# A two-layer backbone step on one core: half of x loaded behind the first modulation weights, and its squares made after h

## The reference

```python
mod = silu(c) @ w_mod[l] + b_mod[l]           # nine vectors of 1024 for each of the two conditionings
sh1, sc1, g1, ... = split(mod, 9)
h = rmsnorm(x, norm_ffn1) * (1 + sc1) + sh1   # rmsnorm divides by sqrt(mean(x*x) + eps)
x = x + 0.5 * g1 * ((silu(h @ w_gate) * (h @ w_up)) @ w_down)   # 1024 -> 2816 -> 1024
...                                           # mixer (Fourier group and attention), second FFN
```

## Time and profile before

| | |
|---|---|
| median of three timed runs | 2757.12 us |
| the profiled execution's own time | 2753.22 us |
| its span, from the first to the last instruction | 2751.1 us |
| mean granted TensorE clock | 0.993 of full |
| TensorE busy | 2676.0 us (97%) |
| VectorE busy | 2095.2 us (76%) |
| ScalarE busy | 1215.2 us (44%) |
| GpSimd busy | 623.1 us (23%) |
| DMA, mean over the span | 99 GB/s |

### The profile page before, as it was taken

The page is one execution under the profiler, slowest core; times in us unless marked ns, Lnnn a source line. Parts: engine busy times, 40 slices in busy tenths (PEclk is TensorE's granted clock), DMA queues, the critical chain, the costliest instruction groups (busy, mean ns, idle before and its releaser), DMA issues. The chain is left out here.

```text
span 2751.1 us, 44480 instructions
## 1 busy us (share of the span) xinstructions
PE 2676.0 (97%) x17686; PEld 2531.2 (92%) x17686; DVE 2095.2 (76%) x2832; ACT 1215.2 (44%) x1998; POOL 623.1 (23%) x323
## 2 busy tenths in 40 slices
PE   5999999999999999999999999999999999999997
PEld 3999999977799999999989999999778999999997
DVE  6978878766566788887988879887665668786876
ACT  5533425556422553343564335255563235443433
POOL 1322412022000123232321413310220003242240
PEclk9999999999999999999999999999999999999998
DMA  6433232210243243423324242312113422222312
GB/s 234 158 121 127 85 123 73 70 59 21 67 138 107 93 160 120 128 101 106 102 98 154 93 139 98 110 62 75 39 37 101 133 80 85 93 72 75 108 47 77
DMA packets 86445, 272.99 MB, mean 99 GB/s; under 512 B 8736, under 2 KB 10016, under 8 KB 86112
## 3 DMA queue, kind: packets, MB, share of 16 engines
q1 hardware_dynamic: 84800, 265.60, 29.2%
q10 hardware_dynamic: 1440, 4.56, 0.4%
HBM read 267.21 MB, written 2.92 MB: 98 GB/s over the span
## 5 line engine op out<-in xcount | busy, mean ns | idle before, releaser
L673 POOL TENSOR_TENSOR sums_raw<-raw_pairs 128x1024 f32<-128x1024 f32 x88 | 239.3, 2720 | 1617.8 <-DVE weights_lo L1771 1035.2
L701 PE MATMUL ps<-h_hi,weights_hi 128*128 128x322 f32 (+1 forms) x1408 | 440.5, 313 | 8.4 <-DVE t_lo L1771 3.1
L705 PE MATMUL ps<-h_hi,weights_lo 128*128 128x322 f32 (+1 forms) x1408 | 437.4, 311 | 0.0
L703 PE MATMUL ps<-h_lo,weights_hi 128*128 128x322 f32 (+1 forms) x1408 | 436.9, 310 | 0.0
L1771 DVE TENSOR_TENSOR weights_lo<-sums_raw,weights_hi 128x1024 fp32r<-128x1024 f32 (+2 forms) x296 | 329.6, 1114 | 57.8 <-ACT weights_hi L1299 26.4
L701 PE MATMUL ps<-t_hi,weights_hi 128*128 128x322 f32 (+1 forms) x1056 | 330.4, 313 | 5.3 <-DVE h_lo L1771 5.3
L701 PE MATMUL ps<-a_hi,weights_hi 128*128 128x320 f32 x1408 | 325.1, 312 | 4.6 <-DVE tmp L1973 3.1
L705 PE MATMUL ps<-t_hi,weights_lo 128*128 128x322 f32 (+1 forms) x1056 | 327.4, 310 | 0.0
L703 PE MATMUL ps<-t_lo,weights_hi 128*128 128x322 f32 (+1 forms) x1056 | 326.3, 309 | 0.0
L705 PE MATMUL ps<-a_hi,weights_lo 128*128 128x320 f32 x1408 | 321.4, 309 | 0.0
L703 PE MATMUL ps<-a_lo,weights_hi 128*128 128x320 f32 x1408 | 321.4, 309 | 0.0
(11 more groups left out here) (283 smaller groups left out, 5718.4 us busy)
## 6 DMA issues: line engine op xcount, KB each, us to landing
raw_pairs<-in_w_up SPq DMA_DIRECT2D x87, 1024.0 KB, 5.0
wm<-in_w_mod SPq DMA_DIRECT2D x72, 512.0 KB, 3.9
raw<-in_w_merge SPq DMA_DIRECT2D x32, 704.0 KB, 4.1
sums_raw<-in_w_down SPq DMA_DIRECT2D x56, 384.0 KB, 3.2
sums_raw<-in_w_down SPq DMA_DIRECT2D x64, 320.0 KB, 2.9
wm<-in_w_mod SPq DMA_DIRECT2D x48, 256.0 KB, 2.9
raw<-in_w_in SPq DMA_DIRECT2D x16, 512.0 KB, 3.5
late_wm<-in_w_mod SPq DMA_DIRECT2D x16, 512.0 KB, 3.5
```

The source lines that it names most:

```text
L673: nc.gpsimd.tensor_tensor(sums_raw[:, UNIT:3 * UNIT].rearrange("p (s c) -> p s c", s=2), w.rearrange("p (s c) -> p s c", s=2)[:, :, 0:UNIT ...
L701: nc.tensor.matmul(out, whi, v, start=first, stop=False)
L703: nc.tensor.matmul(out, whi, v, start=False, stop=False)
L705: mm = nc.tensor.matmul(out, wlo, v, start=False, stop=last)
```

## The change

x is loaded in four parts. Tiles 0, 1 and tiles 4, 5 (the first four in ORDER) are loaded on ScalarE's queue where all of x was; tiles 2, 3 and 6, 7 are loaded on SP's queue between the weights of vector 1 and those of vector 0. The two small tables, which stood there, are loaded behind the weights of vector 0. The late parts of x count on s_raw[1], so that weight_hi adds their 32 to what it waits for; ScalarE waits for them after the fourth tile of h. The squares and adds of the first four tiles are made where all eight were; those of the other four are made by ScalarE and VectorE after the loop that makes h.

```diff
+X_LATE = 2 * 16
...
             for n in range(2 * KT):
                 if n == KT:
-                    sp.dma_start(lat_gain[:], i["lat_gains"]).then_inc(s_const, 16)
-                    sp.dma_start(rope_tab[NOPE:P, :], i["rope"]).then_inc(s_const, 16)
+                    for k in (2, 6):
+                        sp.dma_start(x[:, k:k + 2, :], i["x"][:, k:k + 2]).then_inc(s_raw[1], 16)
                 first_mod_load(n)
+            sp.dma_start(lat_gain[:], i["lat_gains"]).then_inc(s_const, 16)
+            sp.dma_start(rope_tab[NOPE:P, :], i["rope"]).then_inc(s_const, 16)
...
             def weight_hi(g):
                 s, w = g % 2, WIDTHS[g]
-                act.wait_ge(s_raw[s], (g // 2 + 1) * 16)
+                act.wait_ge(s_raw[s], (g // 2 + 1) * 16 + (X_LATE if s else 0))
...
-            act.dma_start(x[:], i["x"]).then_inc(s_x, 16)
+            for k in (0, 4):
+                act.dma_start(x[:, k:k + 2, :], i["x"][:, k:k + 2]).then_inc(s_x, 16)
...
-            act.wait_ge(s_x, 16)
-            for k in range(KT):
+            act.wait_ge(s_x, 16 * 2)
+            for k in range(KT // 2):
                 square(0, k)
...
                 if k == 3:
+                    act.wait_ge(s_raw[1], X_LATE)
                     mod_copy(1)
                 elif k == 4:
                     split_shift(0, 0)
+            for k in range(KT // 2, KT):
+                square(0, k)
...
-            dve.wait_ge(s_x, 16)
-            for k in range(KT):
+            for k in range(KT // 2):
                 add_square(0, k)
...
                     shift_parts(0, 0)
+            for k in range(KT // 2, KT):
+                add_square(0, k)
             dve.wait_ge(s_const, 16 * 2)
```

## The result

| | before | after |
|---|---|---|
| median of 22 timed runs each | 2755.36 us | 2759.89 us |
| ratio, 95% interval | | 1.0016 (1.0010 to 1.0022) |
| profiled execution: own time | 2753.22 us | 2759.67 us |
| its span | 2751.1 us | 2757.6 us |
| mean granted clock | 0.993 | 0.993 |

The changed kernel is slower by 4.5 us, 0.16%, which is outside of chance with so many runs, and within the 0.2% that were called no change (the interval reaches to 0.22%).

A forecast was written before the change was run, and what follows sets the result against it. TensorE bounds the kernel (matmuls in flight for 97% of the span); the early shift sets the end. Held adds +1.6 plus half clock +1.7 gave +3.3 us on the 2757.1 median: 2760.4, range 2755.5 to 2763.

The forecast's parts named there:

- Loads: Start: first vector's last tile at 21.3 instead of 24.65, second vector ended at 36.8, chain through h 3.0 us early.
- The held adds: After the last h_lo: three of four late adds fall into GpSimd's three instructions, over at 58.75.
- Rival (a): Late adds win against GpSimd and end at 55.2; TensorE keeps its clock; -1.2 us, 2755.9; chance 0.12.
- 7.7 us: Late adds' end after GpSimd's start if GpSimd waits for each add too; puts 0.6 us on the sum.
- The sum: Row spreading 1.6 us late by the held adds, plus 1.7 us for the clock: +3.3 us.
- the meeting at 13.47: Kernel before: GpSimd's first-pair work met three adds, over 6.8 us after its start; taken as model for the late adds.
- Where TensorE stands: Ahead of the sum over squares (L734): TensorE waits from 53.9 to 58.8, 4.9 us in one piece.
- the row spreading: L741, at 62.03 before: the point whose shift is the change's worth; expected at 63.6, or 65.3 with half clock.
- The clock: Behind TensorE's stand: 1.2 GHz for 3.4 us at the least, half of it lost: 1.7 us, bounds 0 and 3.4.
- rival (b): Late adds meet GpSimd as worked out, but TensorE's clock holds: +1.6 us, 2758.7; chance 0.2.
- Rival (c): Two stretches of low clock, or lateness growing in the next cycle by 1 to 2 us: 2763; chance 0.1.
- Rival (d): Whole gain of the loads comes through, squares hidden anyway: at most 3.0 to 3.4 us, 2754; chance 0.03.

The follow-up runs named there:

- e6: Kernel before with only the two small tables loaded behind the second vector's weights; 2753.8 us, 1.0000 to before.
- e1: Changed kernel with GpSimd starting the second pair's weight sums only after all eight adds; 2752.5 us, 0.9993 to before.
- e3: Changed kernel with the adds of the last four tiles taking one column of 640; 2757.6 us, 1.0010 to before.
- e7: Changed kernel with the squares of the last three tiles written to PSUM and added from there; 2756.8 us, 1.0010 to before.
- e2: Changed kernel with 32 matmuls whose result nobody reads, put ahead of the first pair's sum over squares; 2755.6 us, 1.0002 to before.
- e4: Changed kernel with the last four tiles' squares and adds put inside the loop that makes h; 2751.6 us, 0.9986 to before.
- e5: Kernel before with its loads, only the last four tiles' squares and adds moved behind the loop making h; 2761.8 us, 1.0026 to before.
- e8: As e4, with the late half of x loaded behind both vectors' weights and late squares and adds spread over tiles five to eight; 2750.9 us, 0.9986 to before.

## Why the prediction was right

**Loads.** Second vector: TensorE ended it at 36.79 (predicted 36.8), the row was copied at 36.91, the last piece of h came 2.9 us early (3.0). The first vector was predicted for 21.3 and came at 20.43. The 0.87 between fits the 0.85 that e6 shows for the tables; it changed nothing, since ScalarE waits for the second vector.

**The held adds.** GpSimd started at 51.78 (51.65) and the adds were over at 58.93 (58.75), 7.15 us later (7.1). e1, e3 and e7 show the mechanism from three sides: no GpSimd, no length; a tiny add, the full wait; an operand in PSUM, no wait. Rival (a) had its adds at 0.82 us and is out.

The rule of the Trainium skill (SBUF — State Buffer, "SBUF: two separate sides"), that the two engines exclude each other for a whole instruction, agrees with the runs on both sides: e3's adds of 2.39 us, and GpSimd's 1.27 against 1.73. That the prediction made 7.7 us of it was an error in what I put in: I took GpSimd's 1.62 us of before as its own duration, but e3 and e7 have 1.27 for the same instruction, so the 1.62 held a wait already. With 1.27 the rule gives 2.39 + 1.27 + 1.27, three times 0.7, and 0.16 between: 7.2, and 7.15 were measured. The sum itself went by the 6.8 us of the meeting at 13.47 and was right because GpSimd's waits are in that figure as well.

**Where TensorE stands.** Predicted 4.9 us, measured 4.81. Without the clock's part, e2 puts the row spreading 2.3 us late in a run whose start was 0.5 late: 1.8, against the 1.6 of the sum.

**The clock.** This is the term that was too small: 1.7 us, for 3.4 us of work at half clock, with 3.4 as bound. The low stretch was 6.8 us long, twice what was taken; TensorE stood in the first 1.4 us of it and worked at the lower level for 5.4, and e2 against the changed kernel gives 2.4 to 2.5 us. That the clock would fall was right: rival (b) is out. In e3 it fell with a stand of 2.78 (half from 56.7 to 63.5), and e7 shows a spell after one of 2.38; in e1, with 1.04, it held.

**The sum.** 1.7 to 1.8 and 2.4 to 2.5 make the 4.2 of the trace; 3.3 were predicted, and the median says 4.5. Rival (c) had the place right where time could still be lost: the low clock did last for two such stretches, but part of it fell into the stand. Its price of 5 to 7 us was not reached in the trace; the median's interval, 2.8 to 6.1, doesn't exclude its lower end. Rival (d), the loads' gain coming through, is what e4 shows for another order of the work: 2.6.

That the forecast time of 2760.4 us was met to 0.5 is in part luck. It was added to a median of three runs that lies 1.8 us above that of 22, and the forecast shift is 1.2 us below the measured one; the two errors partly offset each other.

**The 2.3 us behind L744.** The ten profiled executions side by side go with the clock. The time from the row spreading to the end, against the half clock between 75 and 2725 us:

| | half clock, us | row spreading to end, us |
|---|---|---|
| e1 | 3.4 | 2687.4 |
| before, e4 | 6.8 | 2689.1, 2689.0 |
| e2 | 10.2 | 2688.9 |
| after | 13.6 | 2691.4 |
| e3, e5, e6, e7, e8 | 17 | 2690.9 to 2693.1 |

No kernel was changed there, and no run sets these stretches on purpose, so this is a correlation. The clock is low once more at the end of all ten, for the last 16 to 17 us in the first five of the table and for the last 13 in the other five.

**Not settled.** What decides how many of these stretches an execution gets. And why the median of e1 is 2.5 us below before where its row spreading is no earlier: its profiled execution has one such stretch less than that of before and a span 1.6 us shorter, but no trace of its other ten runs is kept, and the interval includes no difference.

## What to carry to other kernels

Before work is moved out from under a wait, look at what starts on the other engines in the new place: eight adds were free under the weights' transfer, and moving four of them to the point where GpSimd begins cost 7 us, for the most part because they read two operands from SBUF and so wait for GpSimd: with three of the squares in PSUM the row spreading was 3.1 us earlier. A waiting TensorE can cost more than the wait: 4.81 us of standing brought 2.5 us more at half clock. And work that is to be deferred can go into small waits inside the loop (1.7 us of ScalarE's at two places here), which turned +4.5 us into -3.4 with the same loads.

## What the runs showed of the hardware

- A VectorE instruction with both operands in SBUF was held while one of GpSimd's adds from SBUF ran: 0.15 us became 2.39 (e3). With one operand in PSUM it ran at its usual 0.82 us (e7).
- GpSimd waits too. In the first 75 us its 512-column add took 1.26 to 1.27 us where nothing held it (e3, e7, the last one in e1) and 1.6 to 1.8 where VectorE's instructions with two SBUF operands came between.
- Two small tables (165 KB together), issued right behind a row of 512 KB weight tiles, went with a delay of 0.8 us of the last of these tiles: TensorE waited 1.02 to 1.07 us for it, against 0.25 to 0.28 with no table there.
- The half clock did not begin and end with the stand: it was there from 57.6 to 64.4 here, of which 5.4 us held work; in e7 it began at 58.0, 1.2 us after TensorE had resumed, and ended at 61.4.
